# RWKV chunk inverses: whole 64x64 products, or 32x32 diagonal blocks and a corner product

## The chip, the cores and the metric

The kernel runs on one core of a Trainium2 chip as one launch. The metric is the device time of that launch in microseconds. All data are 32-bit floats, and each matrix product of the program shows in the trace as two matmul records with a weight load each.

## The reference

One trunk layer works on 512 latent and 128 context tokens of width 2048. The change touches the RWKV-7 branch: 16 heads of width 64, scanned forward and backward.

```python
def step(s, inp):
    r_t, w_t, k_t, v_t, kk_t, a_t = inp
    sa = jnp.einsum('bhvk,bhk->bhv', s, -kk_t)
    s = (s * w_t[:, :, None, :] + sa[..., None] * (kk_t * a_t)[:, :, None, :]
         + v_t[..., None] * k_t[:, :, None, :])
    return s, jnp.einsum('bhvk,bhk->bhv', s, r_t)
...
y = y + yd
```

Here `s` is a 64x64 state per head and direction. The kernel doesn't step token by token. It cuts the 640 tokens into 10 chunks of 64 and solves each chunk at once, which needs the inverse of a 64x64 unit triangular matrix for each chunk, head and direction. The other parts of the layer (HGRN2 branch, merge, experts, norms) are not touched.

## The kernel before

`stage_rwkv` runs 8 rounds (`PAIRS`), one for each pair of heads; head 0 of the pair sits on partitions 0 to 63 and head 1 on 64 to 127. `heads(out, lhsT, rhs)` issues one product for each head. TensorE's program of a round stands in a fixed order: preparation, `grams` for both directions, `fill(42)`, `inverse`, `fill(52)`, `scan`, then the round's end. `fill(count)` issues that many products of the input projection (`psR<-hT,wrkv`, moving 320 columns), which depend on nothing in the round. They are there to keep TensorE at work while other engines finish. A round has 224 of them.

`grams` works on `GROUPS` of 4, 4 and 2 chunks, so on 6 groups in a round. For each group it computes into PSUM bank 4 `Bc` with both halves of `KR` (128 columns), into bank 5 `Kc` with `KR` (128 columns), into bank 6 `KR` with `Bc` (64 columns), and into bank 7 two transposes (`BK`). VectorE masks the results into `X[:, :, 1]` (M), `Rb`, `Ak`, `Rk` and `X[:, :, 0]` (N); ScalarE copies `BK`; GpSimd adds the identity to M and puts the sum into `X[:, :, 2]` (the running inverse TT).

`inverse` squares M and N and accumulates: in each of 6 levels (`LEV`) it forms for each chunk M·N and N·M (the squares for the next level) and N·TT. Units are (direction, group); unit q uses banks 4 + q%2 and 6 + q%2, so it waits until ScalarE has copied the squares of unit q-2 back to `X` (L726, `inv_copied`) and VectorE has added its third product to TT (L833, `inv_added`):

```python
for i in range(LEV):
    for d in both:
        for k, (c0, n) in enumerate(GROUPS):
            ...
            for c in range(c0, c0 + n):
                if i < LEV - 1:
                    mm = heads(o[:, 0:L], M, N)
                if i < LEV - 2:
                    mm = heads(o[:, L:P], N, M)
                if i:
                    mm = heads(t, N, TT)
```

That is 280 calls of `heads` in a round, 560 products, 1120 matmul records. `scan` then walks the chunks with the finished inverse as a weight.

SyncE loads one 1 MB weight tile (32 fills) at a time into three slots; GpSimd's queue stores gates, states and outputs.

Of the kernel before, what the change touches and what calls it, by code (L numbers as in the profile page):

```python
# [12 lines left out]
P = 128  # L13
# [8 lines left out]
L = 64  # L22
NCH = T // L
HG_HEADS = 8
# [270 lines left out]
def make_masks(nc, pool, s_m, C):  # L295

    n = [0]

    def link(ins):
        n[0] += 1  # L300
        ins.then_inc(s_m, 1)
        pool.wait_ge(s_m, n[0])

    def sel(ap, op, base, pattern, cm):
        link(nc.gpsimd.affine_select(out=ap, in_=ap, compare_op=op, fill=0.0, base=base, pattern=pattern,
                                     channel_multiplier=cm))
# [6 lines left out]
    link(nc.gpsimd.memset(cm[:, 0, :], -1.0))  # L313
    link(nc.gpsimd.memset(cm[:, 2, :], -1.0))
    for h in range(2):
        q = slice(L * h, L * h + L)
        sel(cm[q, 0, :], ALU.is_gt, 0, [[1, L]], -1)
        sel(cm[q, 1, :], ALU.is_ge, 0, [[1, L]], -1)
        sel(cm[q, 2, :], ALU.is_gt, 0, [[-1, L]], 1)
        sel(cm[q, 3, :], ALU.is_ge, 0, [[-1, L]], 1)  # L320
        sel(cm[q, 4, :], ALU.is_gt, 0, [[1, L]], -1)
        sel(cm[q, 5, :], ALU.is_gt, 0, [[-1, L]], 1)
# [81 lines left out]
def stage_rwkv(nc, I, O, S):  # L404


    with ExitStack() as ctx:
# [20 lines left out]
        X = [sb(f"X{d}", [P, NCH, 3, L]) for d in both]  # L428
# [6 lines left out]
        block = ctx.enter_context(nc.Block())  # L435
        g2, lora, ci = S["lw"], S["lora"], C["ci"]
# [6 lines left out]
        UNITS, LEV = len(GROUPS), 6  # L443
# [35 lines left out]
        def _(pool):  # L479
            for r in range(PAIRS):  # L480
# [11 lines left out]
                for d in both:  # L492
                    for g, (c0, n) in enumerate(GROUPS):
                        pool.wait_ge(sem("m_ready"), (2 * r + d) * 3 + g + 1)
                        nc.gpsimd.tensor_tensor(X[d][:, c0:c0 + n, 2, :], X[d][:, c0:c0 + n, 1, :], bcast(ci[:, :], n, 1), ALU.add)\
# [15 lines left out]
        def _(pe):  # L511
# [27 lines left out]

            def grams(r, d):  # L540
                for g, (c0, n) in enumerate(GROUPS):
                    u = (2 * r + d) * 3 + g
                    if u:
                        W("g1_taken", 2 * u)
                    for c in range(c0, c0 + n):
                        mm = heads(cols(4, n, P)[:, c - c0, :], Bc[d][:, c, :], KR[d][:, c].rearrange("p g l -> p (g l)"))
# [6 lines left out]
                    if u:  # L553
                        W("g3_taken", u)
                    for c in range(c0, c0 + n):
                        mm = heads(cols(6, n, L)[:, c - c0, :], KR[d][:, c, 0, :], Bc[d][:, c, :])
# [8 lines left out]
            def inverse(r):  # L565
                last = 6 * (r + 1)
                W("g1_taken", 2 * last)
                W("g2_taken", 2 * last)
                W("g3_taken", last)
                W("bk_taken", last)  # L570
                W("tt_begun", last)
                for i in range(LEV):
                    for d in both:
                        for k, (c0, n) in enumerate(GROUPS):
                            q = (i * 2 + d) * UNITS + k
                            if q >= 2:
                                W("inv_copied", inv_copied(r, q - 2))
                                if inv_added(r, q - 2) > r * INV:
                                    W("inv_added", inv_added(r, q - 2))
                            for c in range(c0, c0 + n):  # L580
                                o, t = cols(4 + q % 2, n, P)[:, c - c0, :], cols(6 + q % 2, n, L)[:, c - c0, :]
                                N, M, TT = (X[d][:, c, m, :] for m in range(3))
                                if i < LEV - 1:
                                    mm = heads(o[:, 0:L], M, N)
                                if i < LEV - 2:
                                    mm = heads(o[:, L:P], N, M)
                                if i:
                                    mm = heads(t, N, TT)
                            mm.then_inc(sem("inv_sums"), 1)

            def scan(r):
                W("inv_copied", INV * (r + 1))
                W("inv_added", INV * (r + 1))
# [7 lines left out]
                for j in range(NCH):  # L601
# [16 lines left out]
                    for d in both:  # L618
                        W(f"nr_ready{d}", 10 * r + j + 1)
                        heads(Sa[d], X[d][:, order[d][j], 2, :], nR[d], start=False, part=True).then_inc(sem(f"sa_sums{d}"), 1)  # L620
# [10 lines left out]
            for r in range(PAIRS):  # L631
# [26 lines left out]
                fill(52)  # L658
# [16 lines left out]
        def _(act):  # L675
# [17 lines left out]
            for r in range(PAIRS):  # L693
# [20 lines left out]
                for d in both:  # L714
                    for g, (c0, n) in enumerate(GROUPS):
                        W("bk_turned", (2 * r + d) * 3 + g + 1)
                        A(BK[d][:, c0:c0 + n].rearrange("p c g l -> p (c g l)"), ps[:, 7, 0:n * P], ACT.Copy).then_inc(sem("bk_taken"), 1)
                for i in (2, 3):
                    take_gate(r, i)
                for i in range(LEV - 1):  # L720
                    for d in both:
                        for k, (c0, n) in enumerate(GROUPS):
# [4 lines left out]
                              ps[:, 4 + q % 2, 0:n * P].rearrange("p (c g l) -> p c g l", c=n, g=2)[:, :, 0:m, :], ACT.Copy)\  # L727
                                .then_inc(sem("inv_copied"), 1)
                if not last:
# [18 lines left out]
        def _(dve):  # L748
# [12 lines left out]
            for r in range(PAIRS):  # L761
# [45 lines left out]
                for d in both:  # L807
                    mNT, mI, mN, mA = (0, 1, 2, 4) if d == 0 else (2, 3, 0, 5)
                    for g, (c0, n) in enumerate(GROUPS):
                        u = (2 * r + d) * 3 + g  # L810
                        cs = slice(c0, c0 + n)
                        G1, G2, G3 = cols(4, n, P), cols(5, n, P), cols(6, n, L)
                        mask = lambda m: bcast(C["cm"][:, m], n, 1)
                        W("g1", u + 1)
                        V.tensor_tensor(X[d][:, cs, 1, :], G1[:, :, 0:L], mask(mNT), ALU.mult).then_inc(sem("m_ready"), 1)
                        W("m_ready", u + 1)
                        dve.sem_inc(sem("g1_taken"), 1)
                        V.tensor_tensor(Rb[d][:, cs, :], G1[:, :, L:P], mask(mI), ALU.mult).then_inc(sem("g1_taken"), 1)
                        W("g2", u + 1)
                        V.tensor_tensor(Ak[d][:, cs, :], G2[:, :, 0:L], mask(mA), ALU.mult).then_inc(sem("g2_taken"), 1)  # L820
                        V.tensor_tensor(Rk[d][:, cs, :], G2[:, :, L:P], mask(mI), ALU.mult).then_inc(sem("g2_taken"), 1)
                        W("g3", u + 1)
                        V.tensor_tensor(X[d][:, cs, 0, :], G3, mask(mN), ALU.mult).then_inc(sem("g3_taken"), 1)
                for i in range(1, LEV):
                    for d in both:
                        for k, (c0, n) in enumerate(GROUPS):
# [4 lines left out]
                            if i > 1 and k == 0:  # L831
                                W("inv_added", inv_added(r, q - 2 * UNITS + UNITS - 1))
                            V.tensor_tensor(X[d][:, c0:c0 + n, 2, :], X[d][:, c0:c0 + n, 2, :], cols(6 + q % 2, n, L), ALU.add)\  # L833
                                .then_inc(sem("inv_added"), 1)
                for d in both:
# [1143 lines left out]
def build_layer(nc, I, O, per=None):  # L1979
    per = per or PER  # L1980
    with ExitStack() as ctx:
        sb = lambda name, shape, dt=F32: ctx.enter_context(nc.sbuf_tensor(name, shape, dt))
        S = {"consts": {"ident": sb("ident", [P, P]), "bd": sb("bdmask", [P, 1, 2, L]), "cm": sb("cmask", [P, 6, L]),
# [83 lines left out]
```

## Time and profile before

| | us |
|---|---|
| three timed runs, median (lowest to highest) | 4825.49 (4823.69 to 4830.38) |
| the profiled execution's own time | 4828.52 |
| its span in the trace | 4826.8 |
| TensorE matmul busy | 4435.6 (92%) |
| VectorE, ScalarE, GpSimd busy | 1457.7, 539.9, 134.8 |

The RWKV rounds take the time from about 304 to 1970 us of the span. TensorE's busy time counts overlapping matmuls once; a matmul record's duration contains its latency, so the distance between the starts of matmuls, not their duration, says what a stream of them costs.

### The profile page before, as it was taken

To read this page: it belongs to the slowest core of one execution; us is meant where nothing else is said; L and a number is where in the kernel's file an instruction comes from. 1 tells how busy PE (TensorE), PEld (TensorE's weight loads), DVE (VectorE), ACT (ScalarE), POOL (GpSimd) and SP (SyncE) were. 2 spreads that over 40 slices of the span, in tenths; PEclk is the share of its full clock that TensorE was granted. 3 is DMA by queue.
4 is the path that set the end of the run, shared out by engine and by line. 5 is a ranking of instruction groups with operands and counts; after the bars stand their busy time and mean duration, and the time that the engine had idled before them with its cause. 6 is when DMAs were issued, how large, how long until landed. Compare 5 with 4: busy or idle time off the path is not lost. (4 is left out here: it accounts for less than half of the span.)

```text
span 4826.8 us, 89082 instructions
## 1 busy us (share of the span) xinstructions
PE 4435.6 (92%) x40577; PEld 2797.0 (58%) x40577; DVE 1457.7 (30%) x2987; ACT 539.9 (11%) x1016; POOL 134.8 (3%) x253
## 2 busy tenths in 40 slices
PE   5899999999999999799999996999996999999995
PEld 2577868687767778577777774554443333333331
DVE  2133342425243333144445554111113111111112
ACT  1021211112112212000101000000011000000001
POOL 0000000000000000100000000000000000000000
PEclk7999999999999999899999996999997999999997
DMA  9111111111111110211111204886126999999997
GB/s 350 46 56 33 48 44 45 47 34 47 41 51 36 57 33 22 74 54 49 48 48 48 57 9 150 272 278 237 61 79 262 372 386 396 397 392 390 386 393 287
DMA packets 412691, 737.94 MB, mean 153 GB/s; under 512 B 16382, under 2 KB 255300, under 8 KB 389444
## 3 DMA queue, kind: packets, MB, share of 16 engines
q1 hardware_dynamic: 405060, 697.65, 40.2%
q0 software_dynamic: 7296, 35.13, 2.7%
q8 instruction: 294, 4.82, 0.4%
q14 instruction: 41, 0.34, 0.0%
HBM read 689.21 MB, written 43.52 MB: 152 GB/s over the span
## 5 line engine op out<-in xcount | busy, mean ns | idle before, releaser
L523 PE MATMUL psR<-hT,wrkv 128*128 128x320 f32 x3584 | 982.3, 435 | 16.4 <-DMA wrkv<-in_w_in 16.4
L523 PEld LDWEIGHTS psR<-hT,wrkv 128*128 128x128 f32 x3584 | 682.2, 191 | 300.7 <-DMA wrkv<-in_w_in 16.9
L1012 PE MATMUL psH<-hT,whg 128*128 128x320 f32 x2560 | 724.8, 439 | 26.1 <-DMA whg<-in_w_in 25.3
L1012 PEld LDWEIGHTS psH<-hT,whg 128*128 128x128 f32 x2560 | 484.5, 193 | 215.0 <-DMA whg<-in_w_in 25.8
L537 PE MATMUL psR<-X 64*64 64x64 f32 x8960 | 286.0, 219 | 7.9 <-ACT X L726 3.4
L1316 PE MATMUL psM<-branches,wmg 128*128 128x512 f32 x512 | 265.2, 600 | 23.4 <-DMA branches<-outr_scratch 23.1
L537 PEld LDWEIGHTS psR<-X 64*64 64x64 f32 x8960 | 272.0, 135 | 24.3 <-ACT X L726 9.4
L1490 PE MATMUL psO<-wout,mergedT 128*128 128x512 f32 x480 | 209.5, 599 | 5.9 <-DMA wout<-in_w_out 5.5
L833 DVE TENSOR_TENSOR X<-X,psR 128x256 f32<-128x256 f32 (+1 forms) x240 | 90.6, 377 | 382.2 <-PE psR L537 380.3
L1876 DVE SCALAR_TENSOR_TENSOR hid<-hid,psE 128x512 f32<-128x512 f32 x16 | 11.0, 687 | 586.7 <-ACT hid L1836 586.7
L1755 PE MATMUL psE<-hT,xg 128*32 128x512 f32 x1392 | 168.1, 601 | 3.8 <-DMA hT<-in_moe_w_up 3.2
L1041 PEld LDWEIGHTS psH<-qs,ks 128*128 128x128 f32 x1120 | 154.2, 208 | 28.0 <-DVE ks L1193 13.7
L1317 PEld LDWEIGHTS psM<-branches,wmg 128*128 128x128 f32 x512 | 97.9, 191 | 123.6 <-issue 123.6
L1041 PE MATMUL psH<-qs,ks 128*128 128x128 f32 x1120 | 159.0, 294 | 9.9 <-DVE ks L1193 9.9
L1755 PE MATMUL psE<-wmore,xg 128*32 128x512 f32 x1376 | 163.4, 593 | 3.4 <-DMA wmore<-in_moe_w_gate 3.4
L1490 PEld LDWEIGHTS psO<-wout,mergedT 128*128 128x128 f32 x480 | 92.0, 192 | 123.4 <-issue 117.0
L1755 PE MATMUL psE<-mergedT,xg 128*32 128x512 f32 x1328 | 157.7, 593 | 4.0 <-DMA mergedT<-in_moe_w_gate 4.0
L726 ACT ACTIVATE X<-psR 128x512 f32<-128x512 f32 (+2 forms) x240 | 116.0, 490 | 167.5 <-PE psR L537 161.5
L1207 DVE TENSOR_TENSOR incl<-incl 128x320 f32<-128x320 f32 x112 | 55.2, 493 | 213.9 <-PE psH L1041 210.6
L1866 DVE TENSOR_TENSOR xg<-psE,A 128x384 f32<-128x384 f32 (+1 forms) x96 | 31.9, 374 | 274.6 <-PE psE L1740 274.6
L1364 DVE SCALAR_TENSOR_TENSOR m<-gth,psM 128x512 f32<-128x512 f32 x32 | 22.0, 688 | 303.0 <-PE psM L1317 303.0
L531 PE MATMUL psR<-lora,lw 128*128 128x320 f32 x160 | 62.9, 545 | 49.3 <-DMA lw<-in_rw_g 49.3
(348 smaller groups left out, 4818.6 us busy)
## 6 DMA issues: line engine op xcount, KB each, us to landing
hT<-in_ada_w SPq DMA_DIRECT2D x64, 1024.0 KB, 8.7
wrkv<-in_w_in SPq DMA_DIRECT2D x56, 1024.0 KB, 5.9
mergedT<-in_moe_w_down SPq DMA_DIRECT2D x46, 1024.0 KB, 20.8
hT<-in_moe_w_gate SPq DMA_DIRECT2D x45, 1024.0 KB, 19.8
wmore<-in_moe_w_up SPq DMA_DIRECT2D x44, 1024.0 KB, 20.2
hT<-in_moe_w_down SPq DMA_DIRECT2D x43, 1024.0 KB, 21.7
hT<-in_moe_w_up SPq DMA_DIRECT2D x42, 1024.0 KB, 19.2
mergedT<-in_moe_w_up SPq DMA_DIRECT2D x42, 1024.0 KB, 19.9
```

The lines of the kernel that those rows point to most:

```text
L523: mm = nc.tensor.matmul(ps[:, 2 * (n % 2) + h, 0:HALF], w[:, n % SLOTS, k, :], S["hT"][:, k, h * HALF:(h + 1) * HALF], start=(k == 0), sto ...
L531: mm = nc.tensor.matmul(ps[:, b + h, 0:HALF], lhsT, rhs[:, h * HALF:(h + 1) * HALF], start=True, stop=True)
L537: mm = nc.tensor.matmul(out[q], lhsT[q], rhs[q], start=start, stop=stop, skip_group_check=part)
L726: A(X[d][:, c0:c0 + n, 0:m, :], ps[:, 4 + q % 2, 0:n * P].rearrange("p (c g l) -> p c g l", c=n, g=2)[:, :, 0:m, :], ACT.Copy)\
L833: V.tensor_tensor(X[d][:, c0:c0 + n, 2, :], X[d][:, c0:c0 + n, 2, :], cols(6 + q % 2, n, L), ALU.add)\
L1012: mm = nc.tensor.matmul(ps[:, 2 * (i % 2) + h, 0:HALF], w[:, i, k, :], S["hT"][:, k, h * HALF:(h + 1) * HALF], start=(k == 0), stop=(k == ...
L1041: mm = nc.tensor.matmul(tok(4 + 2 * (n % 2 == 0), c), ks[d][:, c * P:(c + 1) * P], qs[d][:, c * P:(c + 1) * P], start=True, stop=True)
L1207: lambda: V.tensor_tensor(seg(incl[d][:, :], m, qh), seg(incl[d][:, :], m, qh), wide_t(tq), ALU.mult))
L1316: nc.tensor.matmul(SAMPLE(j, g), lhsT, br[:, g, k, 0:NS], start=(k == 0), stop=(k == PAIRS - 1))
L1317: mm = nc.tensor.matmul(PROMPT(j, g), lhsT, br[:, g, k, NS:T], start=(k == 0), stop=(k == PAIRS - 1))
L1490: mm = nc.tensor.matmul(ps[:, bank(n, t), :], mT[:, k, t * P:(t + 1) * P], w[i % RING][:, k % 2, :], start=(k == 0), stop=(k == KT - 1))
L1755: mm = nc.tensor.matmul(ps[MS * c + 32 * t:MS * c + 32 * t + 32, g, :], xg[e % 2][:, kt, 32 * t:32 * t + 32], w[:, kk * FF + c * 512:kk * ...
```

## The change

M and N keep only the two 32x32 diagonal blocks of each chunk, so a chunk pair has four blocks, on partitions 0 to 31, 32 to 63, 64 to 95 and 96 to 127. The new `blocks` issues one 32x32 product on each. Five levels in place of six suffice for the blocks, and the units become two halves of 5 chunks for each direction. `grams` computes the diagonal blocks apart (`diagonal`), the other gram with 64 columns in place of 128, and in place of the third gram only its off-diagonal corner, which ScalarE copies negated into `Noff`. After the levels the corner of the inverse is TT_near · (Noff · TT_far) for each chunk: one set of products (`y`, and transposes `t`), a copy by ScalarE, a second set, and VectorE's copies into the new `TI`, which `scan` reads. GpSimd copies the diagonal blocks into `TI`. The 52 fills after the levels are split into 6, 6 and 40. The core of the diff (masks of constants, renamed indices and waits that only follow from it are left out):

```diff
-        UNITS, LEV = len(GROUPS), 6
+        HALVES = ((0, 5), (5, 5))
+        UNITS, LEV = len(HALVES), 5
+        near = [[slice(L * h + BL * d, L * h + BL * d + BL) for h in range(2)] for d in both]
+        far = [near[1 - d] for d in both]
...
+                pool.wait_ge(sem("inv_added"), INV * (r + 1))
+                for d in both:
+                    for i in range(4):
+                        q, at = slice(BL * i, BL * i + BL), BL * (i % 2)
+                        nc.gpsimd.tensor_copy(TI[d][q, :, at:at + BL], X[d][q, :, 2, :]).then_inc(sem("ti_diag"), 1)
...
+            def blocks(out, lhsT, rhs):
+                for i in range(4):
+                    q = slice(BL * i, BL * i + BL)
+                    mm = nc.tensor.matmul(out[q], lhsT[q], rhs[q], start=True, stop=True)
+                return mm
+
+            def diagonal(out, lhsT, rhs):
+                for h in range(2):
+                    k = slice(L * h, L * h + L)
+                    for b in range(2):
+                        t = slice(BL * b, BL * b + BL)
+                        mm = nc.tensor.matmul(out[L * h + BL * b:L * h + BL * b + BL], lhsT[k, t], rhs[k, t], start=True, stop=True)
+                return mm
...
                     for c in range(c0, c0 + n):
-                        mm = heads(cols(4, n, P)[:, c - c0, :], Bc[d][:, c, :], KR[d][:, c].rearrange("p g l -> p (g l)"))
+                        diagonal(cols(4, n, BL, 256)[:, c - c0, :], Bc[d][:, c, :], KR[d][:, c, 0, :])
+                        mm = diagonal(cols(4, n, BL, 384)[:, c - c0, :], KR[d][:, c, 0, :], Bc[d][:, c, :])
+                    for c in range(c0, c0 + n):
+                        mm = heads(cols(4, n, L)[:, c - c0, :], Bc[d][:, c, :], KR[d][:, c, 1, :])
...
                     for c in range(c0, c0 + n):
-                        mm = heads(cols(6, n, L)[:, c - c0, :], KR[d][:, c, 0, :], Bc[d][:, c, :])
+                        for h in range(2):
+                            k = slice(L * h, L * h + L)
+                            mm = nc.tensor.matmul(cols(6, n, BL)[far[d][h], c - c0, :], KR[d][k, c, 0, t], Bc[d][k, c, e], start=True, stop=True)
...
                                 if i < LEV - 1:
-                                    mm = heads(o[:, 0:L], M, N)
+                                    mm = blocks(o[:, 0:BL], M, N)
                                 if i < LEV - 2:
-                                    mm = heads(o[:, L:P], N, M)
+                                    mm = blocks(o[:, BL:L], N, M)
                                 if i:
-                                    mm = heads(t, N, TT)
+                                    mm = blocks(t, N, TT)
                             mm.then_inc(sem("inv_sums"), 1)
-
-            def scan(r):
+                fill(6)
                 W("inv_copied", INV * (r + 1))
                 W("inv_added", INV * (r + 1))
+                for k, (c0, n) in enumerate(HALVES):
+                    y, t = cols(4 + 2 * k, n, BL), cols(5 + 2 * k, n, BL)
+                    for c in range(c0, c0 + n):
+                        for d in both:
+                            for h in range(2):
+                                nc.tensor.matmul(y[near[d][h], c - c0, :], Noff[d][far[d][h], c, :], X[d][far[d][h], c, 2, :],
+                                                 start=True, stop=True)
+                        for d in both:
+                            for h in range(2):
+                                mm = nc.tensor.matmul(t[near[d][h], c - c0, :], X[d][near[d][h], c, 2, :], cd[near[d][h], 2, :],
+                                                      start=True, stop=True)
+                    mm.then_inc(sem("far_sums"), 1)
+                fill(6)
+                W("far_taken", UNITS * (r + 1))
+                for c in range(NCH):
+                    mm = blocks(cols(6, NCH, BL)[:, c, :], YT[:, c, 1, :], YT[:, c, 0, :])
+                mm.then_inc(sem("corner"), 1)
+
+            def scan(r):
+                W("ti_diag", 8 * (r + 1))
+                W("ti_corner", 4 * (r + 1))
...
                 inverse(r)
-                fill(52)
+                fill(40)
                 scan(r)
```

Two places of TensorE's order show how the products move. The first is a group of four chunks in `grams` (round 0, forward). Before, the group's own rows are these (the last two repeat for the other chunks):

```order
L537 MATMUL psR<-KR0,Bc0 64x128 [waits rw_factors,rw_kk_max,rw_v_taken]
L537 MATMUL psR<-KR0,Bc0 64x128 x7
L537 MATMUL psR<-KR0,Kc0 64x128 x8
L537 MATMUL psR<-Bc0,KR0 64x64 x8
L537 MATMUL psR<-cident,Bc0 64x64 x2
L537 MATMUL psR<-cident,Kc0 64x64 x2
```

Of the change the same group reads (the second and third rows stand four times, once for each chunk):

```order
L572 MATMUL psR<-KR0,Bc0 32x32 [waits rw_factors,rw_kk_max,rw_v_taken]
L572 MATMUL psR<-KR0,Bc0 32x32 x3
L572 MATMUL psR<-Bc0,KR0 32x32 x4
...
L558 MATMUL psR<-KR0,Bc0 64x64 x8
L558 MATMUL psR<-KR0,Kc0 64x128 x8
L597 MATMUL psR<-Bc0,KR0 32x32 x8
L558 MATMUL psR<-cident,Bc0 64x64 x2
L558 MATMUL psR<-cident,Kc0 64x64 x2
```

The group went from 40 products to 72, and its stream now alternates between 64x64 weights and weights of 64 rows and 32 columns: four changes of shape in a group. The second place is the end of the levels (round 0), where the scan's first product (`cident,s0`) stood right behind the 52 fills. Of the change it reads:

```order
L564 MATMUL psR<-X1 32x32 [waits rw_inv_added,rw_inv_copied]
L564 MATMUL psR<-X1 32x32 x19
L544 MATMUL psR<-hT,wrkv 128x320 x6
L641 MATMUL psR<-X0,Noff0 32x32 [waits rw_inv_added,rw_inv_copied]
...
L645 MATMUL psR<-cdiag,X1 32x32 x2
L544 MATMUL psR<-hT,wrkv 128x320 x6
L564 MATMUL psR<-X0 32x32 [waits rw_far_taken]
L564 MATMUL psR<-X0 32x32 x39
L544 MATMUL psR<-hT,wrkv 128x320 x14
...
L558 MATMUL psR<-cident,s0 64x64 [waits rw_s0_in,rw_ti_corner,rw_ti_diag]
```

The corner's two sets of products stand between the fills, each behind six of them, and the scan now waits for GpSimd's and VectorE's copies into `TI`.

## Rows read from the trace of the kernel before

**Rows 1.** The page: busy time, share, count; then slices of TensorE and clock.

```profile
PE 4435.6 (92%) x40577; PEld 2797.0 (58%) x40577; DVE 1457.7 (30%) x2987; ACT 539.9 (11%) x1016; POOL 134.8 (3%) x253
...
PE   5899999999999999799999996999996999999995
...
PEclk7999999999999999899999996999997999999997
```

**Rows 2.** Windows: third round's grams, fills, inverse, fills, scan, rest; last round's inverse, scan.

```profile
core 0: us, PE busy (x) PEld busy (x) DVE busy (x) ACT busy (x) POOL busy (x), PEclk, DMA share, GB/s
746.00:762.00 16.00, 16.00 (x402) 15.91 (x401) 9.52 (x30) 2.77 (x5) 3.81 (x6) 1.00 0.01 3
762.00:784.70 22.70, 22.70 (x84) 15.79 (x84) 0.21 (x2) 1.79 (x3) 1.10 (x2) 1.00 0.27 80
784.70:821.40 36.70, 35.71 (x1122) 34.05 (x1121) 11.03 (x29) 14.49 (x30) 0.00 (x0) 1.00 0.10 30
821.40:849.50 28.10, 28.10 (x105) 19.62 (x104) 0.29 (x1) 0.70 (x1) 0.00 (x0) 1.00 0.14 38
849.50:876.40 26.90, 23.71 (x642) 20.65 (x641) 13.50 (x61) 5.00 (x22) 0.00 (x0) 1.00 0.01 3
876.40:967.60 91.20, 84.27 (x339) 58.74 (x337) 44.79 (x63) 18.67 (x27) 3.76 (x7) 0.94 0.22 61
1890.40:1927.20 36.80, 35.75 (x1121) 34.02 (x1120) 11.04 (x29) 15.19 (x31) 0.55 (x1) 1.00 0.04 13
1927.20:1954.50 27.30, 23.87 (x641) 20.73 (x640) 13.79 (x62) 5.00 (x22) 0.00 (x0) 1.00 0.01 3
```

**Rows 3.** Line 537's matmuls: shortest, median, longest duration in ns; first and last start.

```profile
L537 PE MATMUL psR<-X x8960: 213/218/268, 342.4 to 1927.0; 64*64 64x64 f32 x200
L537 PE MATMUL psR<-KR,Bc x640: 269/269/320, 303.7 to 1869.5; 64*64 64x128 f32 x160
```

**Rows 4.** TensorE's timeline, third round: fills, then grams (start, length, matmuls).

```profile
744.31 1.78 PE L523 MATMUL psR<-hT,wrkv 128*128 128x320 f32 x6
746.02 1.09 PE L537 MATMUL psR<-KR,Bc 64*64 64x128 f32 x16
...
749.22 1.04 PE L537 MATMUL psR<-KR,Bc 64*64 64x128 f32 x16
750.09 1.04 PE L537 MATMUL psR<-KR,Kc 64*64 64x128 f32 x16
750.97 0.63 PE L537 MATMUL psR<-Bc,KR 64*64 64x64 f32 x16
```

**Rows 5.** TensorE's timeline in a later stage: weights of 128 columns, then of 32.

```profile
3655.73 0.94 PE L1461 MATMUL psO<-diag,xrows 128*128 128x128 f32 x7
3656.60 1.08 PE L1475 MATMUL psO<-hT,wr 128*32 128x128 f32 x32
```

**Rows 6.** Waits in the third round's inverse (total us, times, longest).

```profile
DVE X L833 <- PE psR L537: 47.9, 25, 29.7
ACT X L726 <- PE psR L537: 20.5, 20, 3.6
PEld psR L537 <- ACT X L726: 1.2, 4, 0.4
PEld psR L537 <- issue: 0.9, 3, 0.4
```

**Rows 7.** Groups by form, 300 to 1960 us: ScalarE and VectorE in the inverse.

```profile
L726 ACT ACTIVATE X<-psR 128x512 f32<-128x512 f32 x128 | 76.4, 597 | 137.9 <-PE psR L537 137.9
L726 ACT ACTIVATE X<-psR 128x256 f32<-128x256 f32 x96 | 36.7, 383 | 28.1 <-PE psR L537 23.3
...
L833 DVE TENSOR_TENSOR X<-X,psR 128x256 f32<-128x256 f32 x160 | 67.5, 422 | 365.0 <-PE psR L537 364.1
...
L833 DVE TENSOR_TENSOR X<-X,psR 128x128 f32<-128x128 f32 x80 | 23.1, 288 | 17.2 <-PE psR L537 16.2
```

**Rows 8.** Groups by form, 300 to 1960 us: GpSimd.

```profile
L495 POOL TENSOR_TENSOR X<-X,cident 128x256 f32<-128x256 f32 x32 | 23.2, 726 | 170.9 <-DVE X L815 170.9
...
L495 POOL TENSOR_TENSOR X<-X,cident 128x128 f32<-128x128 f32 x16 | 7.3, 455 | 29.6 <-DVE X L815 29.6
```

**Rows 9.** The page: its first line, and the instruction queue (packets, MB, share of 16 engines).

```profile
span 4826.8 us, 89082 instructions
...
q8 instruction: 294, 4.82, 0.4%
```

More of the change, by code:

```diff
@@ L23 @@
 NCH = T // L
+BL = L // 2
 HG_HEADS = 8
@@ L312, in make_masks @@
     link(nc.gpsimd.memset(cm[:, :, :], 1.0))
-    link(nc.gpsimd.memset(cm[:, 0, :], -1.0))
-    link(nc.gpsimd.memset(cm[:, 2, :], -1.0))
     for h in range(2):
         q = slice(L * h, L * h + L)
[L317 to L322, printed above, removed]
+        sel(cm[q, 0, :], ALU.is_ge, 0, [[1, L]], -1)
+        sel(cm[q, 1, :], ALU.is_ge, 0, [[-1, L]], 1)
+        sel(cm[q, 2, :], ALU.is_gt, 0, [[1, L]], -1)
+        sel(cm[q, 3, :], ALU.is_gt, 0, [[-1, L]], 1)
+    cd = C["cd"]
+    link(nc.gpsimd.memset(cd[:, 0:2, :], -1.0))
+    link(nc.gpsimd.memset(cd[:, 2, :], 0.0))
+    for i in range(4):
+        q = slice(BL * i, BL * i + BL)
+        sel(cd[q, 0, :], ALU.is_gt, 0, [[1, BL]], -1)
+        sel(cd[q, 1, :], ALU.is_gt, 0, [[-1, BL]], 1)
+        link(nc.gpsimd.affine_select(out=cd[q, 2, :], in_=cd[q, 2, :], compare_op=ALU.not_equal, fill=1.0, base=0,
+                                     pattern=[[-1, BL]], channel_multiplier=1))
     link(nc.gpsimd.memset(C["ci"][:, :], 0.0))
@@ L427, in stage_rwkv @@
         Bc, Kc, Ak, Rb, Rk = ([sb(f"{n}{d}", [P, NCH, L]) for d in both] for n in ("Bc", "Kc", "Ak", "Rb", "Rk"))
-        X = [sb(f"X{d}", [P, NCH, 3, L]) for d in both]
+        X = [sb(f"X{d}", [P, NCH, 3, BL]) for d in both]
+        Noff = [sb(f"Noff{d}", [P, NCH, BL]) for d in both]
+        TI = [sb(f"TI{d}", [P, NCH, L]) for d in both]
+        YT = X[0]
         etot = [sb(f"etot{d}", [P, NCH]) for d in both]
@@ L494, in _ @@
                         pool.wait_ge(sem("m_ready"), (2 * r + d) * 3 + g + 1)
[L495 removed]
+                        nc.gpsimd.tensor_tensor(X[d][:, c0:c0 + n, 2, :], X[d][:, c0:c0 + n, 1, :], bcast(cd[:, 2, :], n, 1), ALU.add)\
                             .then_inc(sem("tt_begun"), 1)
@@ L538, in heads @@
                 return mm
+            def blocks(out, lhsT, rhs):
+                for i in range(4):
+                    q = slice(BL * i, BL * i + BL)
+                    mm = nc.tensor.matmul(out[q], lhsT[q], rhs[q], start=True, stop=True)
[7 more added lines that the diff above has]
+                return mm
             def grams(r, d):
@@ L566, in inverse @@
                 last = 6 * (r + 1)
-                W("g1_taken", 2 * last)
+                W("g1_taken", 3 * last)
                 W("g2_taken", 2 * last)
-                W("g3_taken", last)
+                W("noff_taken", 2 * last)
                 W("bk_taken", last)
@@ L619, in scan @@
                         W(f"nr_ready{d}", 10 * r + j + 1)
-                        heads(Sa[d], X[d][:, order[d][j], 2, :], nR[d], start=False, part=True).then_inc(sem(f"sa_sums{d}"), 1)
+                        heads(Sa[d], TI[d][:, order[d][j], :], nR[d], start=False, part=True).then_inc(sem(f"sa_sums{d}"), 1)
                     for d in both:
@@ L721, in _ @@
                     for d in both:
-                        for k, (c0, n) in enumerate(GROUPS):
+                        for k, (c0, n) in enumerate(HALVES):
                             q = (i * 2 + d) * UNITS + k
@@ L807, in _ @@
                 for d in both:
-                    mNT, mI, mN, mA = (0, 1, 2, 4) if d == 0 else (2, 3, 0, 5)
+                    mI, mA = d, 2 + d
                     for g, (c0, n) in enumerate(GROUPS):
@@ L832, in _ @@
                                 W("inv_added", inv_added(r, q - 2 * UNITS + UNITS - 1))
-                            V.tensor_tensor(X[d][:, c0:c0 + n, 2, :], X[d][:, c0:c0 + n, 2, :], cols(6 + q % 2, n, L), ALU.add)\
+                            V.tensor_tensor(X[d][:, c0:c0 + n, 2, :], X[d][:, c0:c0 + n, 2, :], cols(6 + q % 2, n, BL), ALU.add)\
                                 .then_inc(sem("inv_added"), 1)
+                if r == 0:
+                    W("ti_zeroed", 2)
+                W("corner", r + 1)
+                for d in both:
+                    for q in near[d]:
+                        V.tensor_copy(TI[d][q, :, BL * (1 - d):BL * (1 - d) + BL], cols(6, NCH, BL)[q]).then_inc(sem("ti_corner"), 1)
                 for d in both:
```

42 lines of the change are left out of this document (28 added, 14 removed).

## The prediction

> **What bounds the kernel now.** I read the page first: TensorE is busy 92% of the span, VectorE 30%, at the high clock nearly throughout [rows 1]. Then I cut one round into windows. In grams, fills, inverse, fills and scan TensorE is busy for 16.0 of 16.0 us, 22.7 of 22.7, 35.7 of 36.7, 28.1 of 28.1 and 23.7 of 26.9, all at a granted clock of 1.00, the 2.4 GHz level [rows 2]. The stages stand in a row on TensorE. The fills are a fixed 224 a round, so a microsecond that the inverse saves on TensorE is one less in the round, unless something else becomes late. The inverse's matmuls run from 342 to 1927 us, in 8 rounds [rows 3], at 36.7 to 36.8 us each [rows 2]: 294 us in all. That is the most that the change could touch there.
>
> Is this stretch limited by matmuls or by waits? The longest waits are those of VectorE and ScalarE for TensorE; TensorE's own add up to about 2 us [rows 6]. So it is the stream of matmuls that sets it, and the question is the price of a step in that stream.
>
> **The price of a step.** The two heads' matmuls sit on different quarters of the array and run together, so I count pairs. 16 matmuls of 64 columns take 0.63 us from the first start to the last end; the last lasts 0.218 [rows 3], so 8 pairs are 7 steps in 0.41 us: 59 ns a step [rows 4]. 560 such steps are 33.0 us of the 36.7; the other 3.7 are stalls and shape changes. 16 matmuls of 128 columns take 1.04, the last 0.269: 110 ns a step [rows 4]. So 64 columns fewer save 51 ns, and on that line 32 columns cost 59 - 25.5 = 33 ns a step.
>
> In the change a step is four matmuls, one per diagonal block. Do four run together? In a later stage weights of 32 columns are used four across: 32 matmuls of 128 columns in 1.08 us, the last 0.27, are 8 steps of four, (1.08 - 0.27)/7 = 116 ns each [rows 5], near the 110 of a pair with the same columns. So four tiles side by side do share a step. What no row shows is four tiles fed as fast as one step in 33 ns. The bounds for the step q: from below 29 ns (half of 59, nothing fixed in a step); from above 116 ns, the densest feeding that a row shows (29 ns a matmul and its weights), if that is already the limit of feeding. I take 33: the rows at 110 and 116 are explained by their 128 columns alone, so nothing yet points to a limit of feeding. Its chance is priced below.
>
> **Part by part, per round.**
>
> *Levels.* Removed: 560 pair steps, 36.7 us with stalls. Added: 880 products (11 calls of four blocks for 20 chunks and directions), 440 steps of four: 0.44 × 33 = 14.5 us. Stalls: a unit may start when unit q-2 has been copied. A copy of 320 columns lies between 383 ns for 256 and 597 for 512 [rows 7], so about 0.43 us, and an add of 160 between 288 for 128 and 422 for 256, about 0.32. With some 0.3 us for the way from the last matmul to ScalarE and back this is 0.74. A unit of three products per chunk is 30 steps, 0.99 us: no stall. Units with two are 0.66 us: 0.1 us in every second. The last level's units (0.33 us) wait some 0.3 each. Together about 2.0 us (bounds: nothing, and the 3.7 of now). So 16.5 in place of 36.7: -20.2.
>
> *Grams.* Per chunk and direction, before: 110 + 110 + 59 × 2, as each product is two records: 2 × 110 + 2 × 110 + 2 × 59 + 4 × 59 = 794 ns, 15.9 us for 20, as the window has it [rows 2]. After: 4 steps of four diagonal blocks (4 × 33), 2 × 59, 2 × 110, the corner's 2 pair steps of 32 columns (2 × 33), 4 × 59: 772 ns, 15.4 us. VectorE, ScalarE and GpSimd have more small work or less large, and stay behind TensorE as now (9.5, 2.8 and 3.8 us busy of 16 [rows 2]).
>
> *Changes of shape.* 24 more in a round's grams. From 128x128 to 64x64: six fills take 1.78 us, so 0.27 a step, and the next matmul starts 0.36 us after the last fill's start: 0.09 more, and the first group of 16 then takes 1.09 in place of 1.04 [rows 4]: 0.14. From 128 columns to 32: seven matmuls in 0.94 us, steps of 0.11, and the next starts 0.20 after the last start: 0.09 [rows 5]. No row shows 64x64 to 64x32; bounds 0 and 0.25, I take 0.12, near both rows: 2.9 us. The Trainium skill (TensorEngine Tiling (Array Packing), Key Properties) says that a change of tiling mode, not of the tile alone, drains TensorE; rows 4 and 5 show such a cost at 0.09 to 0.14 us, and by either I would pay for these changes. So grams: -0.4 + 2.9 = +2.5.
>
> *Corner.* 160 + 80 records are 60 steps: 2.0 us, and four changes of shape, 0.6. Three covers: six fills (12 records of 0.27 [rows 4], 3.2 us) hide the last add and its way; the next six hide ScalarE's two copies (0.43 each); 40 fills (21.4 us) hide VectorE's four copies into `TI` and GpSimd's eight. GpSimd's adds of 256 and 128 columns cost 0.73 and 0.46 us [rows 8], so a copy of 320 is at most 0.86, eight are under 7 us. Corner: +2.6. The fills themselves cost nothing new, 6 + 6 + 40 = 52. No load is late: each stage's DMA share is 0.27 or less [rows 2], and the SyncE queue follows the fills.
>
> *The last round* has no fills left: its inverse ends at 1927.2 and the scan follows at once [rows 2]. There GpSimd's copies stand bare, about 6.5 us in place of the 2.6: +3.9 once. Scan and the rest of the round are untouched.
>
> Sum: 8 × (-20.2 + 2.5 + 2.6) + 3.9 = 8 × (-15.1) + 3.9 = -117 us. Against the profiled execution's 4828.5 that is 4711.5; that execution lies 3 us above the median, so 4709 there.
>
> As a function of the step, a round changes by 0.62 q - 35.6 us (0.44 levels, 0.06 corner, 0.12 grams, q in ns). It is even at q = 57: everything hangs on whether four matmuls and four weight loads can be fed in less than that.
>
> **Rivals.**
>
> 1. *TensorE's instructions arrive no faster than now.* Eight instructions a step (four loads, four matmuls) come in place of four. If the 29 ns per matmul and load of rows 5 are the limit of the feed and not of the array, a step is 116 ns; the corner pairs in grams are then two matmuls, so 0.60 q - 35.6 = +34 us a round, 8 × 34 + 4 = +276: 5101 us. For it: no stretch in the trace feeds denser; the inverse's 59 ns per pair is also 29 per matmul. Against it: both equal what their columns explain, and 64 and 128 columns differ by 51 ns at the same number of instructions. It decides from q = 57 up. The Trainium skill (TensorE: Matmul & The Clock Gate, Part 1, the section on 56 ns against 53.3 ns) states that starts never come closer than about 25 ns however few the columns; by that, as an estimate, q is 100, a round loses 0.60 × 100 - 35.6 = 24 us and the time is about 5025. Trace and rule don't collide, as 29 ns is above it; but it was given for matmuls in a row, and here the question is four tiles.
>
> 2. *The instruction fetch stretches the steps.* The instruction queue moved 294 packets in 0.4% of 16 engines' span [rows 9], so 0.4% × 16 × 4826.8 / 294 = 1.05 us a packet. 4.82 MB / 294 is 16.4 kB, and 4.82 MB for 89,082 instructions [rows 9] are 54 bytes each, so a packet holds some 300, 38 steps of four: 28 ns a step if packets follow each other without a gap, just under my price, so hardly a reserve. With gaps half as long as a packet q is 42 and a round gains 9.6 us: 4752 us. With gaps as long as the packet q is 56 and nothing is gained; with gaps of one and a half it is 70, and a round loses 7.8: 4892. Against it: during the fills the queue needs little, so some may be stored ahead.
>
> 3. *The clock falls.* Four 32x32 blocks fill a quarter of the array, two 64x64 half of it. At the 1.2 GHz level, half of the other, a step would be about 66 ns (an estimate, twice 33), and a round loses 5.3 us: 4871. Against it: the scan, with fewer matmuls in its 26.9 us than the inverse per microsecond (642 against 1122 in 36.7), keeps 1.00 [rows 2].
>
> 4. *Nothing changes*, because another chain sets the round. Then 4825. Against it: TensorE's idle time in a round of 221 us is a few us in the rest and the scan [rows 2], and the other engines wait for it.
>
> **How the numbers follow.** My forecast (q from 29 to 40, shape changes 0 to 0.25 us) has a chance of 0.60: 4709 - 20 - 28 at the one end, 4709 + 35 + 29 at the other, so 4660 to 4775. A partial gain beyond that (q up to 55, by rival 2) gets 0.13, 4775 to 4817. About even 0.04. Rival 1, with rival 2's worse half, 0.19, from 4840 to 5101; the clock 0.04. So faster 0.73, same 0.04, slower 0.23 (0.2% is about what a measurement here can tell from no change). The range that leaves out no more than 2 in 10 reaches over the partial gain to the nearer losses: 4660 to 4860; the forecast's own is 4660 to 4775.
>
> **What would show it.** Four blocks' matmuls should start within some 25 ns, and the next four 33 ns after the first; 120 records (one unit of the second level, 30 steps) should take near 1.0 us where as many, 60 pair steps, now take 3.5. The window of the levels should be 16 to 17 us, grams 18 to 19, between the fills 2 us of corner products, no wait of TensorE for GpSimd outside the last round. Wrong would be: even spacing of 25 ns or more between all matmuls (rival 1), gaps once in some 256 instructions (rival 2), a granted clock under 1.00 in the levels (rival 3).

## The result and the profile after

The changed kernel takes 4986.57 us (median of 4 runs, 4982.39 to 4995.31) where the kernel before took 4826.59 in the same comparison: a ratio of 1.0333, 95% interval 1.0315 to 1.0351. It is 160 us slower; the forecast was 4709 us, in a range from 4660 to 4860.

The page of the changed kernel, its first line, TensorE's row, the slices of the granted clock and the instruction queue, answers to [rows 1] and [rows 9]:

```profile
span 4993.6 us, 108161 instructions
...
PE 4420.8 (89%) x50177; PEld 2752.0 (55%) x50177; DVE 1413.9 (28%) x2907; ACT 503.7 (10%) x1016; POOL 155.1 (3%) x327
...
PEclk7998898989898989789999997999998999999997
...
q8 instruction: 369, 6.05, 0.5%
```

TensorE is busy for a smaller share of a longer span, and the granted clock falls again and again all through the rounds. There are 19,079 more instructions and 75 more packets of the instruction queue; 75 x 256 is 19,200, so a packet carries 256 instructions.

The windows of the third round answer to [rows 2], with the same columns: grams, fills, levels, the next fills with the corner's first products, its last product and the fills behind it, scan, rest.

```profile
786.40:805.40 19.00, 18.92 (x722) 16.86 (x721) 8.48 (x30) 5.11 (x15) 2.45 (x6) 1.00 0.02 4
805.40:828.20 22.80, 22.80 (x90) 15.89 (x90) 0.00 (x0) 2.10 (x5) 1.10 (x2) 1.00 0.28 81
828.20:878.90 50.70, 25.89 (x1761) 24.15 (x1760) 4.83 (x15) 6.46 (x16) 0.00 (x0) 0.53 0.08 23
878.90:889.20 10.30, 10.30 (x190) 7.00 (x184) 0.32 (x1) 0.87 (x2) 3.57 (x8) 0.81 0.01 3
889.20:911.80 22.60, 22.60 (x163) 15.94 (x162) 1.95 (x4) 0.70 (x1) 0.00 (x0) 1.00 0.18 48
911.80:938.60 26.80, 23.62 (x642) 20.57 (x641) 13.44 (x61) 4.95 (x21) 0.00 (x0) 1.00 0.01 4
938.60:1029.50 90.90, 83.75 (x342) 58.53 (x339) 44.84 (x63) 18.72 (x27) 3.76 (x7) 0.96 0.22 61
```

The round is 243.1 us long, it was 221.6. Grams give 3.0 of the 21.5, the two windows behind the levels (32.9 against 28.1) 4.8, and the levels 14.0: 50.7 where the whole products took 36.7 and the forecast said 16.5. In them TensorE is busy for only half the time. The other seven rounds are alike: the levels of all eight sum to 387.0 us, 48.4 each.

What does TensorE wait for there? The waits in the third round's levels (total us, times, longest) answer to [rows 6]:

```profile
DVE X L903 <- PE psR L564: 68.8, 16, 35.6
ACT X L793 <- PE psR L564: 42.9, 16, 4.2
PEld psR L564 <- issue: 26.9, 14, 3.5
PE psR L564 <- issue: 24.8, 13, 3.4
```

VectorE and ScalarE wait for TensorE; TensorE waits for "issue", which is to say for nothing that the profile shows, 13 times, 24.8 us in all. The timeline of the first stops (start, length, matmuls, idle time before):

```profile
828.16 1.75 PE L564 MATMUL psR<-X 32*32 32x32 f32 x176
833.33 1.93 PE L564 MATMUL psR<-X 32*32 32x32 f32 x128 [3.42 <-issue]
836.81 1.93 PE L564 MATMUL psR<-X 32*32 32x32 f32 x128 [1.55 <-issue]
840.56 1.93 PE L564 MATMUL psR<-X 32*32 32x32 f32 x128 [1.82 <-issue]
```

After a first piece of 176 matmuls the pieces hold 128, each with its weight load: 256 instructions, one packet. From 833.33 to the end of the levels, 45.6 us, 3520 - 352 = 3168 instructions pass, 12.4 packets: 3.7 us a packet. The DMA view of 828 to 845 us, in 40 slices of 0.425 us, shows when the packets come:

```profile
GB/s 342 337 323 299 351 360 376 0 0 0 0 0 0 0 0 39 0 0 0 0 0 0 0 39 0 0 0 0 0 0 0 0 39 0 0 0 0 0 0 0
...
q8 instruction: 4, 0.07, 1.5%
```

39 GB/s over a slice are 16.6 kB, one packet; between them nothing is moved. The three slices begin at 834.4, 837.8 and 841.6 us, 1.0 to 1.1 us after TensorE went on at 833.33, 836.81 and 840.56 (over all pieces of these levels it is 1.0 to 1.7 us); it goes on with the next piece 2.4 to 2.8 us later again. So a packet starts after the piece before it has begun and before that piece, of 1.93 us, has ended. This fits a packet that is asked for only when the piece before it begins, and whose way takes some 3.7 us; the asking itself is in no record. A piece that TensorE is done with sooner ends in a stop.

How much lies ahead when the levels begin differs from round to round: the first piece holds 168 to 272 matmuls, so 336 to 544 instructions with their loads. The longest is that of the last round:

```profile
2035.78 2.57 PE L564 MATMUL psR<-X 32*32 32x32 f32 x272
```

The Trainium skill (Runtime: NRT & Kernel Launch, Instruction fetch mechanics) says that instructions come in blocks of 256, and the trace agrees (pieces of 128 matmuls with 128 loads). It also gives TensorE a store of 2048 instructions and says that the fetch is mostly hidden; here the first stop came after 336 to 544, and about half of the levels is waiting for the next packet.

### The profile page after: what moved, and what is told of

Read it like the earlier page. It is cut to its first block and busy times, and to the rows that moved or that the text cites. A ratio compares the mean times of both kernels' runs of the same rounds, so it can differ in the third digit from the quotient of the medians.

```text
span 4993.6 us, 108161 instructions
## 1 busy us (share of the span) xinstructions
PE 4420.8 (89%) x50177; PEld 2752.0 (55%) x50177; DVE 1413.9 (28%) x2907; ACT 503.7 (10%) x1016; POOL 155.1 (3%) x327
## 5 line engine op out<-in xcount | busy, mean ns | idle before, releaser
L544 PE MATMUL psR<-hT,wrkv 128*128 128x320 f32 x3584 | 996.3, 438 | 15.9 <-DMA wrkv<-in_w_in 15.9
L544 PEld LDWEIGHTS psR<-hT,wrkv 128*128 128x128 f32 x3584 | 687.2, 193 | 302.0 <-DMA wrkv<-in_w_in 16.4
L564 PE MATMUL psR<-X 32*32 32x32 f32 x14720 | 214.0, 230 | 182.5 <-issue 182.0
L564 PEld LDWEIGHTS psR<-X 32*32 32x32 f32 x14720 | 198.4, 143 | 202.9 <-issue 201.9
L903 DVE TENSOR_TENSOR X<-X,psR 128x160 f32<-128x160 f32 x128 | 41.2, 322 | 527.7 <-PE psR L564 527.7
L1942 DVE TENSOR_TENSOR xg<-psE,A 128x384 f32<-128x384 f32 (+1 forms) x96 | 31.9, 374 | 274.3 <-PE psE L1816 274.3
L1257 DVE COPY_PREDICATED att<-hmask,psH 128x640 f32<-128x640 int32 x120 | 103.1, 859 | 0.0
```

What stands on the lines that cost most here:

```text
L544: mm = nc.tensor.matmul(ps[:, 2 * (n % 2) + h, 0:HALF], w[:, n % SLOTS, k, :], S["hT"][:, k, h * HALF:(h + 1) * HALF], start=(k == 0), sto ...
L564: mm = nc.tensor.matmul(out[q], lhsT[q], rhs[q], start=True, stop=True)
L1257: did(V.copy_predicated(att[:, :, :], i32(bcast(hm[:, mask, :], TT, 1)), wide(b).rearrange("p (c t) -> p c t", t=P)), "att_taken")
```

## The experiments

The kernel before has a median of 4829.18 us in the comparisons of e1 to e4 and 4828.67 in those of e5 to e7.

**e1: more instructions for the same work.** The kernel before, with each product of 64 columns issued as two of 32:

```diff
-                                if i < LEV - 1:
-                                    mm = heads(o[:, 0:L], M, N)
...
+                                for s in (slice(0, L // 2), slice(L // 2, L)):
+                                    if i < LEV - 1:
+                                        mm = heads(o[:, 0:L][:, s], M, N[:, s])
...
```

> The kernel before, with each 64-column product of the levels issued as two products of 32 columns: the same arithmetic and the same columns, twice the instructions (4480 instead of 2240 a round), still 64x64 weights, two tiles, no change of shape. Theory S (supply): TensorE's instructions come in blocks of 256 and a block takes 3.4 to 3.9 us to come, whatever it holds; 17.5 blocks are 60 to 68 us a round in place of 36.7, so the program takes about 5020 to 5070 us, with gaps of TensorE every 256 instructions. Theory A (the array: four small tiles are what is slow): 1120 pair steps at 33 ns are 37 us, no change, 4815 to 4850.

Measured: 5064.57 us, ratio 1.0485 (1.0464 to 1.0506). The number came as supply would have it, but the trace does not show it. The window of the third round's levels:

```profile
845.80:912.00 66.20, 66.06 (x2242) 65.87 (x2241) 10.99 (x29) 14.72 (x30) 0.00 (x0) 1.00 0.07 19
```

TensorE is busy all through. Its timeline from 846 us on shows a single piece:

```profile
845.83 16.35 PE L537 MATMUL psR<-X 64*64 64x32 f32 x554
```

There is no stop. 554 matmuls are 277 pairs in 16.35 us, 59 ns a pair, as with 64 columns [rows 4]: a pair of 64x64 products does not get shorter below 64 columns. 1120 such pairs alone make the 66 us. So e1 came out for another reason and decides nothing between the theories. It gives two bounds: 256 instructions each 3.78 us (64 steps of 59 ns) still come without a stop, and the kernel before, with the same 59 ns, was within a few per cent of the 3.7 us all along.

**e2: fewer columns, as many instructions.** The changed kernel with 8 of 32 moving columns in the levels' products, and in the copies and adds behind them; the inverses are incomplete. The third of three products stands for all:

```diff
+                                s = slice(0, 8)
...
-                                    mm = blocks(t, N, TT)
+                                    mm = blocks(t[:, s], N, TT[:, s])
```

> The changed kernel, with 8 in place of 32 moving columns in every product of the levels (the copies and adds take 8 columns too; the inverses are then incomplete): the same number of instructions, a quarter of the columns. Theory S, with a block that is asked for when the one before begins and takes about 3.7 us to come: the levels stay at 45 to 51 us a round, the program at 4960 to 5000 us. S with a block that is asked for only when the one before is used up: a burst shorter by about 1 us shortens each block, levels 35 to 40 us, program near 4900. Theory A (array or clock sets the levels): levels under 25 us, program under 4800.

Measured: 5007.88 us, one run, a little above what supply would have. The window of the third round's levels:

```profile
834.20:885.80 51.60, 25.21 (x1762) 24.04 (x1761) 2.94 (x15) 3.67 (x16) 0.00 (x0) 0.53 0.08 24
```

And pieces on TensorE's timeline in it:

```profile
839.97 1.89 PE L564 MATMUL psR<-X 32*32 32x8 f32 x128 [4.08 <-issue]
843.72 1.89 PE L564 MATMUL psR<-X 32*32 32x8 f32 x128 [1.86 <-issue]
```

A quarter of the columns, and the levels stay at 51.6 us, with the same pieces of 128. Neither the columns nor ScalarE's and VectorE's work (3.67 and 2.94 us busy, where it was 6.46 and 4.83) sets them. The pieces did not get shorter either, 1.89 us against 1.93, so the run says nothing on whether a packet is asked for when a piece begins or when it ends.

**e3: some fills between the pieces.** The changed kernel with 40 of a round's 94 fills moved into the levels, two behind each unit.

```diff
+                            fill(2)
...
-                fill(42)
+                fill(36)
                 inverse(r)
-                fill(40)
+                fill(6)
```

> The changed kernel, with 40 of a round's 94 fills around the levels moved in between the units, two behind each of the 20 units (36 before, 40 inside, 6, 6, 6 behind). Theory S: the fills run while instructions come; levels with their 40 fills take (3520 + 160) / 256 x 3.7 = 53 us, where levels alone took 48 and the 40 fills 22: about 20 us a round less, program 4800 to 4850 us, near the kernel before, and a granted clock in the levels well above 0.53. Theory A: the fills add their own time and 40 changes of shape, 5000 us or more.

Measured: 4895.03 us, ratio 1.0130 (1.0113 to 1.0147). The window of the third round's levels with their fills:

```profile
800.80:855.40 54.60, 44.25 (x1838) 30.82 (x1837) 4.81 (x15) 7.16 (x17) 0.55 (x1) 1.00 0.18 49
```

Busy is 44.25 of 54.60, at a clock of 1.00. TensorE's timeline in it, fills (L544) and levels (L564):

```profile
817.56 1.34 PE L544 MATMUL psR<-hT,wrkv 128*128 128x320 f32 x4
818.84 1.17 PE L564 MATMUL psR<-X 32*32 32x32 f32 x115
820.94 0.25 PE L564 MATMUL psR<-X 32*32 32x32 f32 x5 [0.94 <-issue]
821.13 1.34 PE L544 MATMUL psR<-hT,wrkv 128*128 128x320 f32 x4
```

The levels' window came near what was expected (3520 instructions and 160 of the fills are 14.4 packets, 3.8 us each), and the stops are shorter and fall inside the units. The total came out 45 us above the 4850 expected: from one round's levels to the next it is 225 to 230 us, against 219 to 222 before, as grams and corner cost what they did and the levels with 40 fills are still bound by supply; and the last round, which has no fills left behind its fourth gate tile, keeps its stops.

**e4: the change's arithmetic without small tiles in the levels.** Five levels on the diagonal blocks and the corner product, but each product of the levels a whole 64x64 one with zeros in the off-diagonal blocks: 880 records in the levels in place of 1760, and of 1120 before. Grams stay those of the kernel before, the corner's products are 32x32 as in the change. VectorE masks the blocks and writes the corner into `X`; GpSimd has no copies.

```diff
-        UNITS, LEV = len(GROUPS), 6
+        UNITS, LEV = len(GROUPS), 5
...
-                        V.tensor_tensor(X[d][:, cs, 1, :], G1[:, :, 0:L], mask(mNT), ALU.mult).then_inc(sem("m_ready"), 1)
+                        V.tensor_tensor(X[d][:, cs, 1, :], G1[:, :, 0:L], within(d), ALU.mult).then_inc(sem("m_ready"), 1)
```

> The algorithm of the change (five levels on the diagonal blocks, then the corner) in the kernel before's form: the blocks lie in 64x64 matrices whose off-diagonal corners are zero, and the levels use whole 64x64 products, so 1760 instructions a round in place of 3520 (and of 2240 before). Grams as before; the corner is written into the same matrix, without GpSimd's copies. Theory S and the price of a pair step (59 ns) agree: 440 pair steps are 26 us, 6.9 blocks of instructions 25 us, levels 27 to 29 us with stalls and no gaps every 256 instructions; with the corner's 2.6 us and some more work on VectorE in grams a round gains 5 to 7 us on the kernel before: 4770 to 4790 us. If the blocks as such were the trouble (five levels, corner, waits), it would be slower than before.

Measured: 4798.51 us, ratio 0.9934 (0.9917 to 0.9950): faster than both kernels, 9 us above the range expected. Windows of the third round's grams and levels:

```profile
737.00:752.90 15.90, 15.90 (x401) 15.82 (x400) 11.96 (x39) 2.77 (x5) 3.81 (x6) 1.00 0.02 3
...
775.70:804.80 29.10, 28.23 (x882) 26.79 (x881) 8.74 (x23) 11.33 (x24) 0.00 (x0) 1.00 0.13 38
```

Grams are as before, the levels 7.6 us shorter for 240 records fewer, and the corner gives part of it back; from one round's levels to the next 4.4 us are left on average, and none in the last round, where no fills cover the corner. So the arithmetic with one level fewer is worth having, and the loss comes with the small tiles.

**e5: fewer instructions, as many columns.** The changed kernel with the two products of a level that share their weights N issued as one of 64 columns: 1440 records in place of 1760. ScalarE's copy and VectorE's add now read one bank, so the copy waits for the add.

```diff
-                                if i < LEV - 2:
-                                    mm = blocks(o[:, BL:L], N, M)
-                                if i:
-                                    mm = blocks(t, N, TT)
+                                m0, m1 = (1 if i < LEV - 2 else 2), (3 if i else 2)
+                                mm = blocks(o[:, BL * m0:BL * m1], N, X[d][:, c, m0:m1, :].rearrange("p m l -> p (m l)"))
...
+                            if i:
+                                W("inv_added", inv_added(r, q))
```

> The kernel after the change, but with the two products of a level that share their weights N (N times M and N times TT) issued as one product of 64 columns in place of two of 32: 9 block calls per chunk and direction in place of 11, so 1440 records and 2880 instructions in a round's levels in place of 1760 and 3520, with the same columns in all. Theory S (TensorE's instructions arrive 256 at a time, one such block each 3.7 us at the most): 2880 / 256 = 11.25 blocks, 41 to 43 us for the levels in place of 48, and about 4930 us in all (8 rounds, some 7 us less in each). Rival (a fixed stall per unit of the levels, by its waits for ScalarE and VectorE; the units stay 20): 47 to 51 us for the levels and 4975 to 5000 us, or more, since ScalarE's copy here waits for VectorE's add.

Measured: 4918.40 us, ratio 1.0188 (1.0171 to 1.0205). Windows of the levels, third round and the sum over all eight:

```profile
809.90:849.10 39.20, 25.55 (x1442) 23.44 (x1441) 4.83 (x15) 6.46 (x16) 0.00 (x0) 0.59 0.09 28
...
sum 317.70, PE 204.22 PEld 189.97 DVE 38.60 ACT 52.41 POOL 0.55; mean PE 25.53 PEld 23.75 DVE 4.83 ACT 6.55 POOL 0.07
```

39.7 us a round in place of 48.4: 0.82 of the time for 0.82 of the instructions, at the same columns and with one more wait; that is a little less than the 41 to 43 expected. The rival, a stall of fixed size per unit, is out.

**e6: the same, with the fills spread over the levels.** e5, with 56 of the 94 fills ahead of the units. ScalarE's take of the fourth gate tile moves behind the unit at which that tile is done.

```diff
+        FILLS = (3, 3, 3, 3, 2)
...
+                            fill(FILLS[i])
...
-                fill(42)
+                fill(14)
                 inverse(r)
-                fill(40)
+                fill(12)
...
+                            if q == 10:
+                                take_gate(r, 3)
```

> e5 with 56 of a round's 94 fills moved into the levels, 3 ahead of each unit (2 in the last level), 14 ahead of the levels, 6 and 6 around the corner and 12 behind it. Theory S: levels and their fills hold 2880 + 224 instructions, 12.1 blocks of 3.7 us or 45 us, and TensorE has about 30.5 us of fills and 15 of small matmuls and 4 of shape changes in them, 49 to 51 us in all; so the supply is just enough, the stretch from the end of the grams to the scan is about 73 us where it was 88 before the change, grams 3 us longer, a round gains 10 to 12 us in seven rounds, and the last round, which has few fills left, loses some 10: 4750 to 4775 us. Rival (the small matmuls stall by themselves, whatever is mixed in between): the levels keep their 40 us and the fills come on top, about 4930 us as for e5.

Measured: 4767.98 us, ratio 0.9873 (0.9857 to 0.9889): the fastest of all, 61 us under the kernel before and 219 under the changed one. Windows of the third round (grams, 14 fills, levels with fills, corner with fills):

```profile
727.80:746.60 18.80, 18.72 (x722) 16.72 (x721) 8.39 (x30) 5.11 (x15) 2.45 (x6) 1.00 0.02 4
746.60:755.90 9.30, 9.30 (x36) 6.33 (x34) 0.00 (x0) 1.40 (x4) 0.55 (x1) 1.00 0.51 150
755.90:804.80 48.90, 48.90 (x1548) 33.96 (x1547) 4.81 (x15) 7.09 (x17) 0.55 (x1) 1.00 0.13 36
804.80:820.60 15.80, 15.80 (x290) 11.08 (x290) 2.27 (x5) 1.47 (x3) 3.57 (x8) 1.00 0.21 56
```

TensorE is busy for 48.90 of 48.90 us in the levels, at a clock of 1.00. Its timeline there, levels (L565) and fills (L545):

```profile
766.42 1.08 PE L565 MATMUL psR<-X 32*32 32x32 f32 x80
767.43 1.88 PE L545 MATMUL psR<-hT,wrkv 128*128 128x320 f32 x6
769.24 1.08 PE L565 MATMUL psR<-X 32*32 32x32 f32 x80
```

The small matmuls that stood half the time run without a stop: a unit and its fills are 86 matmuls, 172 instructions, in 2.82 us, so 256 take 4.2, longer than a packet's 3.7. Grams' end to scan is 74.0 us, where [rows 2] have 22.7 + 36.7 + 28.1 = 87.5.

**e7: the fills spread, the products not joined.** The changed kernel with 60 fills in the levels, `FILLS = (3, 4, 4, 3, 1)`, 12 ahead, 10 behind; ScalarE's take of the fourth gate tile moves as in e6, behind another unit.

> The kernel after the change with 60 of a round's 94 fills moved into the levels (3 or 4 ahead of each unit, 1 in the last level), 12 ahead, 6 and 6 around the corner, 10 behind; the products stay 11 calls. Theory S: levels and fills hold 3520 + 240 instructions, 14.7 blocks of 3.7 us, 54 to 57 us with their fills; a round gains some 6 to 8 us against before in seven rounds and the last loses about 19: 4785 to 4805 us. Rival (stalls independent of what is mixed in): about 4985 us.

Measured: 4819.79 us, ratio 0.9980 (0.9970 to 0.9990). The window of the third round's levels with fills:

```profile
762.80:817.40 54.60, 53.12 (x1876) 37.50 (x1875) 4.82 (x15) 7.05 (x17) 0.55 (x1) 1.00 0.18 49
```

1.5 us of stops are left, and the whole is hardly faster than the kernel before. TensorE's timeline in it:

```profile
770.67 0.89 PE L565 MATMUL psR<-X 32*32 32x32 f32 x80
771.49 2.42 PE L545 MATMUL psR<-hT,wrkv 128*128 128x320 f32 x8
773.84 1.22 PE L565 MATMUL psR<-X 32*32 32x32 f32 x120
```

The units of 80 and of 120 matmuls give the price of a step (below). The third round is as expected, 54.6 us; the total is 15 us above the bound given: this mix stands just at the limit (54.6 us for 14.7 packets), and other rounds fell over it; from one round's levels to the next it is 214 to 224 us, in e6 211 to 216.

## Why the prediction was wrong

The step that failed is the levels' 0.44 x 33 = 14.5 us with stalls of 2.0, and behind it the choice to give rival 2 no more than gaps of one and a half packets. Where stalls of 2.0 were put, the third round has 24.8 us of stops for the next packet. Levels took 48.4 us in place of 16.5, 8 x 31.9 = 255 us. The median missed the forecast by 278 us, the profiled execution, from which these terms come, by 286.

- *The step itself.* In e7 40 more matmuls, 10 steps of four, add 1.22 - 0.89 = 0.33 us: 33 ns, the price taken. That is luck as far as the runs show, since the line that gave it does not hold for what it was drawn from: a pair of 64x64 with 32 columns costs 59, not 33 (e1). The Trainium skill (TensorE: Matmul & The Clock Gate, the section on 56 ns against 53.3 ns) has starts no closer than about 25 ns; four tiles in 33 ns are one each 8, so that does not hold across tiles. Rival 1, as an even spacing of 25 ns or more, is out. Its size was right all the same, as an average over a long stretch: 3.7 us for 256 instructions are 29 ns for a matmul and its load.
- *The feed.* Rival 2 named the cause and sized it wrong. I took the time of a packet (1.05 us) for most of a packet's turn and thought in gaps of half to one and a half; the turn is 3.7 us, a gap of two and a half. A packet holds 256 instructions, not some 300, which came of dividing the queue's bytes by all instructions of the page. In its own terms q becomes 3.7 us / 32 steps = 115 ns, all but rival 1's 116, and 0.44 x 115 = 50.6; the grams' and the corner's short stretches are largely spared it. "Some may be stored ahead" held for 336 to 544 instructions of 3520.
- *The clock.* Rival 3 saw a fall in the levels, and 0.53 is what stood there, but as a consequence: with the stops shorter (e3) or away (e6) it is 1.00 with the same tiles. It does not set the levels' time, since the stops take up what a piece leaves of a packet's 3.7 us: e3, at 1.00, has 3.8 a packet too. Its cost lies behind them: the first 12 fill matmuls, at 878.91, take 5.45 us, where six take 1.78 and so 12 some 3.4 in [rows 4]: 2.0 us here, 1.1 to 2.4 in the seven rounds with such fills, 13 us in all. Their row on the timeline of the changed kernel:

```profile
878.91 5.45 PE L544 MATMUL psR<-hT,wrkv 128*128 128x320 f32 x12
```

No fill matmul behind them is as slow (the next window has 1.00).

- *Grams.* 19.0 against 16.0 + 2.5 in the third round: the changes of shape are about as dear as taken. But this round's grams are the shortest of the eight, and the only ones without a stop; all eight take 157.7 us, 10 more than 8 x 18.5. Feed is in it here too, as in the last round's 20.8 us:

```profile
PE psR L558 <- issue: 1.0, 1, 1.0
PE psR L572 <- issue: 0.5, 1, 0.5
```

- *Corner.* 4.8 us longer behind the levels, less 2.0 of the clock: 2.8, forecast 2.6; over the seven rounds 1 us more than forecast. GpSimd's copies (3.57 us for eight) were hidden.
- *Last round.* From the levels' end to the scan 9.4 us, forecast 2.6 + 3.9; the scan after it 28.3 in place of 27.3, at a clock of 0.93. Their windows in the changed kernel:

```profile
2081.00:2090.40 9.40, 3.71 (x240) 3.21 (x241) 2.27 (x5) 0.87 (x2) 3.57 (x8) 0.50 0.01 3
2090.40:2118.70 28.30, 25.32 (x640) 22.12 (x640) 13.53 (x61) 5.00 (x22) 0.00 (x0) 0.93 0.01 3
```

TensorE is busy for 3.71 of the 9.40 us. What stands bare there is not GpSimd's copies, as the prediction had it:

```profile
2081.41 3.98 POOL L519 COPY TI<-X 32x320 f32<-32x320 f32 x8 [43.96 <-DVE X L903]
2087.04 1.18 PE L564 MATMUL psR<-X 32*32 32x32 f32 x71 [1.38 <-issue]
2088.27 2.04 DVE L910 COPY TI<-psR 32x320 f32<-32x320 f32 x4 [6.93 <-PE psR L564]
2090.42 0.70 PE L558 MATMUL psR<-cident,s 64*64 64x64 f32 x8 [2.20 <-issue]
```

GpSimd is done at 2085.4. The corner's second products are split by a stop and end at 2088.2; only then do VectorE's four copies run, 2.04 us, and the scan's first product comes right behind them.

In all 255 + 13 + 10 + 1 + 4 is 283 of the profiled execution's 286 us.

What stays open: what asks for a packet, and what the 1.0 us before it starts and the time between its landing and TensorE's next instruction consist of. The records show when, not why, and no run changed the way of the fetch itself.

## What to carry to other kernels

Before cutting matmuls into smaller tiles, count instructions as well as columns: beyond the 336 to 544 that lay ahead here, a stretch needs some 3.7 us for every 256 of them, loads included, so 14.5 ns each; and the densest stretch of a trace (here 59 ns for four) shows what is known to work, not that there is room below it. Where a dense stretch stands beside work with long instructions, mix the two so that every 256 instructions last that long, and join products that share their weights: in e6 that turned the loss of 3.3% into a gain of 1.3%. A stop put down to "issue", in pieces of equal count, is the sign of it.

## What the hardware showed that was not expected

- Of the changed kernel's levels 336 to 544 instructions were there ahead, no more than 352 in the third round even after 22 us of fills in which TensorE took only 180; after that, one packet of 256 came each 3.7 us.
- Four 32x32 fp32 products of 32 columns run in 33 ns together; a pair of 64x64 takes 59 ns with 32 as with 64 columns.
- In the change's levels the granted clock was 0.53, near the 1.2 GHz level, with TensorE standing half the time (25.89 us busy of 50.70); in e1, busy throughout, and in e3 and e6, with fills among the same small tiles, it was 1.00.
